# Seven block products for eight in w_out and w_down, and the norms behind them with half tiles between the transposes

## The reference

```python
merged = (jax.nn.sigmoid(ga) * jnp.einsum("bsc,cd->bsd", attn, w_attn_branch[l])
          + jax.nn.sigmoid(gc) * jnp.einsum("bsc,cd->bsd", conv, w_conv_branch[l]))
h = h + jnp.einsum("bsd,de->bse", merged, w_out[l])
hn = rms_norm(h, ffn_norm[l])
up = causal_depthwise_conv(jnp.einsum("bsd,df->bsf", hn, w_up[l]), ffn_conv_w[l])
gate, val = jnp.split(up, 2, axis=-1)
h = h + jnp.einsum("bsf,fd->bsd", jax.nn.silu(gate) * val, w_down[l])
return rms_norm(h, final_norm)
```

## Time and profile before

| what | value |
|---|---|
| runs | 1052.18, 1052.56, 1054.4 us, median 1052.56 |
| span of the profiled execution | 1050.5 us |
| time of the profiled execution around its span | not listed; the median of the runs is 2.06 us above the span |
| PE busy | 1038.4 us |
| DVE busy | 593.9 us |
| ACT busy | 445.9 us |
| POOL busy | 51.0 us |
| DMA traffic | 107.08 MB |

### The profile page before, as it was taken

One profiled execution on the slowest core, in us unless ns is written; L12 is line 12 of the kernel. 1 busy time (PEld: TensorE's weight loads), 2 busy tenths in 40 slices (PEclk: granted clock), 3 DMA queues, 4 the chain that ended last, 5 costly groups with the idle time before them and its releaser, 6 DMA issues.

```text
span 1050.5 us, 13952 instructions
## 1 busy us (share of the span) xinstructions
PE 1038.4 (99%) x5453; PEld 846.1 (81%) x5453; DVE 593.9 (57%) x1110; ACT 445.9 (42%) x855; POOL 51.0 (5%) x71
## 2 busy tenths in 40 slices
PE   9999999999999999999999999999999999999997
PEld 7877778888888888888888888899888677777785
DVE  6466665445356666533466563553456673567757
ACT  5355542233345434431234442453244454556640
POOL 0000000000001100000000000125200001000000
PEclk9999999999999999999999999999999999999999
DMA  7421133222341842333122323334211222511012
GB/s 277 160 65 57 61 101 100 95 89 98 123 140 41 275 152 87 98 125 110 61 101 85 100 97 110 131 122 135 91 61 61 61 81 71 211 41 41 21 61 80
DMA packets 29106, 107.08 MB, mean 102 GB/s; under 512 B 3227, under 2 KB 3371, under 8 KB 28401
## 3 DMA queue, kind: packets, MB, share of 16 engines
q1 hardware_dynamic: 24864, 86.13, 24.8%
q0 software_dynamic: 4032, 19.96, 5.3%
q10 hardware_dynamic: 144, 0.10, 0.0%
HBM read 101.44 MB, written 7.36 MB: 104 GB/s over the span
## 4 chain that ended last, share of the span: by engine, by line
PE 88%; DVE 5%; ACT 4%; issue 2%; DMA 2%; DVEq 0%; SPq 0%; ACTq 0%
PE ps L780 26%; PE ps L782 25%; PE ps L781 25%; PE ps L1054 2%; PE ps L1222 2%; PE ps L1205 1%; PE ps L1187 1%; DMA raw<-wp 1%; ACT whi L1285 1%; PE ps L1143 1%; PE ps L1106 1%; ACT SC L1336 1%; PE ps L1175 1%; DVE wlo L1633 0%; DVE SC L1739 0%
## 5 line engine op out<-in xcount | busy, mean ns | idle before, releaser
L780 PE MATMUL ps<-XH,whi 128*128 128x512 f32 (+1 forms) x864 | 336.7, 390 | 0.6 <-DVE XL L1646 0.2
L782 PE MATMUL ps<-XH,wlo 128*128 128x512 f32 (+1 forms) x864 | 326.9, 378 | 0.0
L781 PE MATMUL ps<-XL,whi 128*128 128x512 f32 (+1 forms) x864 | 326.5, 378 | 0.0
L1633 DVE TENSOR_TENSOR wlo<-raw,whi 128x1024 fp32r<-128x1024 f32 (+1 forms) x158 | 191.6, 1218 | 166.7 <-ACT whi L1285 166.1
L1285 ACT CAST whi<-raw 128x1024 fp32r<-128x1024 f32 (+1 forms) x158 | 161.2, 1027 | 95.9 <-PE ps L782 70.5
L780 PEld LDWEIGHTS ps<-XH,whi 128*128 128x128 f32 x864 | 162.6, 188 | 43.0 <-issue 12.4
L782 PEld LDWEIGHTS ps<-XH,wlo 128*128 128x128 f32 x864 | 162.6, 188 | 31.2
L781 PEld LDWEIGHTS ps<-XL,whi 128*128 128x128 f32 x864 | 162.8, 188 | 27.8 <-issue 0.5
L780 PE MATMUL ps<-whi,GH 128*128 128x512 f32 x176 | 68.8, 391 | 0.0
L782 PE MATMUL ps<-whi,GL 128*128 128x512 f32 x176 | 68.5, 389 | 0.0
L781 PE MATMUL ps<-wlo,GH 128*128 128x512 f32 x176 | 68.5, 389 | 0.0
(11 more groups left out here) (305 smaller groups left out, 1333.1 us busy)
## 6 DMA issues: line engine op xcount, KB each, us to landing
raw<-wp SPq DMA_DIRECT2D x150, 512.0 KB, 3.5
vec_dram<-row_dram POOLq DMA_DIRECT2D x1, 3072.0 KB, 13.7
H<-x POOLq DMA_DIRECT2D x1, 2048.0 KB, 8.1
x_dram<-H POOLq DMA_DIRECT2D x1, 2048.0 KB, 8.8
A<-w1c POOLq DMA_DIRECT2D x2, 1024.0 KB, 6.3
A<-x_dram POOLq DMA_DIRECT2D x1, 2048.0 KB, 12.8
y<-A SPq DMA_DIRECT2D x8, 256.0 KB, 2.0
raw<-wp SPq DMA_DIRECT2D x4, 402.0 KB, 3.9
```

What stands on the lines that cost most here:

```text
L780: self.e.matmul(o, ah, bh, start=start, stop=False)
L781: self.e.matmul(o, ah, bl, start=False, stop=False)
L782: return self.e.matmul(o, al, bh, start=False, stop=stop)
L1633: self.e.tensor_tensor(wlo[BUF[i]][:, 0:w], raw[i % NR][:, 0:w], whi[BUF[i]][:, 0:w].bitcast(F), ALU.subtract).then_inc(sems["lo"], 1)
```

## The change

The product of w_out (group 0) and that of w_down, now in three groups of 8, 8 and 6 feature tiles (groups 1, 2, 3), are each cut into 2 x 2 blocks: token halves, alternate feature tiles, column halves. By a scheme with seven block products in place of eight, the operands of some products are sums of blocks. DVE makes the sums of activations in halves of 256 tokens (`sums_of`), ACT and DVE split them into MW or GW, which hold seven operands. The sums of weight blocks come from accumulating DMAs that POOL issues into X and Y buffers (`wino_sums`); products 0, 3 and 4 take their blocks from SP's ring as before. The order of operand and target of each product is in `OPERAND`, `WBANKS`, `INTO`; products 2, 4 and 5 go on accumulating in the banks of 0, 1 and 2, and DVE adds or subtracts the bank to H behind each (behind product 5 to two parts of it).

In the groups with a norm (0 and 3), rows 0 and 1 are complete after product 4, the second column half of rows 2 and 3 after product 5, and the first after product 6. Their norms and transposes stand between the halves of products 5 and 6; behind product 6 the half tile of up slot 0, the transposes of row block 2, the half tile of slot 1, the transposes of row block 3 and the half tile of slot 2 alternate. whi and wlo have five buffers in turn here, and some more at the norms. In SBUF, Y0 (group 0) lies on the first half of XL.

The diff, cut to its core (memory layout, semaphore counts and the packing of weights on the host are left out):

```diff
+N_UNITS = 14
+SLOT_FFN = SLOT_WOUT + N_UNITS
+TILES_OF = [0, 8, 8, 6]
+PAIRS = [4, 4, 4, 3]
+FIRST_F = [0, 0, 8, 16]
+UNIT0 = [SLOT_WOUT] + [SLOT_FFN + 2 * (FIRST_F[G] + TILES_OF[G]) + N_UNITS * (G - 1) for G in (1, 2, 3)]
+LAST_G = 3
+SLOT_B2 = UNIT0[LAST_G] + N_UNITS
...
+OPERAND = [0, 4, 5, 1, 6, 3, 2]
+WBANKS = [(6, 7), (3, 0), (6, 7), (4, 5), (3, 0), (6, 7), (4, 5)]
+INTO = [(0, 0), (1, 1), (0, 1), (0, 0), (0, 1), (1, 1), (1, 0)]
+BEFORE = [(1, 3), (1, 5), (1, 4), (0, 0), (0, 2), (0, 1), (0, 5)]
...
+def added(G, p, r):
+
+    return 16 * G + (2 * p + r + 1 if p < 5 else 12 + 2 * r if p == 5 else 15 + r)
...
 def weave(main, *lanes):
@@ -226,19 +272,46 @@
     def slot(i):
         en.split_all(min(i + 3, N_SLOTS))
 
-    def rows_normed(m, rows):
-        for t in range(3):
-            rows(t)
-            if t == 2:
-                en.turn(m, 0)
-            en.norm_rest(m, t)
+    def product(G, p):
+        u = unit(G, p, 0)
+        en.split_all(u + 4)
+        en.wino(G, p, 0)
+        en.split_all(u + 5)
+        en.wino(G, p, 1)
+
+    def group(G):
+        product(G, 0)
+        product(G, 1)
+        en.wino_sums(G, 2)
+        product(G, 2)
+        en.wino_sums(G, 3)
+        product(G, 3)
+
+    def group_normed(G, m):
+        group(G)
+        product(G, 4)
+        u = unit(G, 6, 0)
+        en.split_all(u + 2)
+        en.eps_on(m, 0)
+        en.eps_on(m, 1)
+        en.wino(G, 5, 0)
+        en.norm_rest(m, 0)
+        en.wino(G, 5, 1)
+        en.norm_rest(m, 1)
+        en.eps_on(m, 2)
+        en.eps_on(m, 3)
+        en.split_all(u + 4)
+        en.wino(G, 6, 0)
+        en.turn(m, 0)
         en.turn(m, 1)
-        rows(3)
+        en.split_all(u + 5)
+        en.wino(G, 6, 1)
+        en.norm_rest(m, 2)
         en.norm_rest(m, 3)
-        en.turn(m, 2)
 
     def first_three(m, i, tile, tiles):
         en.part(i, 0, 0)
+        en.turn(m, 2)
         en.part(i, 1, 0)
         en.turn(m, 3)
         en.part(i, 2, 0)
@@ -306,50 +379,59 @@
     weave(conv(), (attention(), 0, 19 / 24))
     en.lower()
     for n in range(8):
+        if n == 5:
+            en.wino_sums(0, 0)
         for j in range(2):
             slot(SLOT_GATE + 3 * n + j)
             en.gate(n, j)
+            if j == 0 and n and n % 2 == 0:
+                for part in range(2):
+                    en.merge_sums(n // 2 - 1, part)
         slot(SLOT_GATE + 3 * n + 2)
         for j in range(2):
             en.branch(n, j)
+        if n == 7:
+            en.begin_norm(1)
+            en.wino_sums(0, 1)
         en.merge(n)
-
-    en.begin_norm(1)
-    for c in range(2):
-        for g in range(4 if c == 0 else 2):
-            slot(SLOT_WOUT + 4 * c + g)
-            if c == 1 and g == 1:
-                en.split_all(SLOT_FFN + 2)
-            for t in range(4):
-                en.wout(c, g, t)
-    en.split_all(SLOT_FFN + 3)
-    rows_normed(1, lambda t: en.wout(1, 3, t))
+    for part in range(2):
+        en.merge_sums(3, part)
+
+    group_normed(0, 1)
 
...
     en.ffn()
-    for half in range(2):
-        for j in range(11):
-            if half == 0 and j == 0:
-                first_three(1, SLOT_FFN, en.up, [(0, 0, 0, 2), (0, 0, 1, 2), (0, 1, 0, 2)])
+    for G in (1, 2, 3):
+        last = FIRST_F[G] + TILES_OF[G] - 1
+        for f in range(FIRST_F[G], last + 1):
+            if f == last - 2:
+                en.wino_sums(G, 0)
+                en.wino_sums(G, 1)
+            if f == 0:
+                first_three(1, SLOT_FFN, en.up, [(0, 0, 2), (0, 1, 2), (1, 0, 2)])
                 en.distances()
             else:
-                for g in range(1 if half == 0 and j == 1 else 0, 2):
-                    slot(SLOT_FFN + half * N_HALF + 2 * j + g)
-                    en.up(half, j, g, 0)
-                    en.up(half, j, g, 1)
-            en.glu(half, j)
-            if half == 0 and j == 10:
+                for g in range(1 if f == 1 else 0, 2):
+                    slot(up_slot(f, g))
+                    if f == last and g == 1:
+                        en.split_all(unit(G, 1, 1) + 1)
+                    en.up(f, g, 0)
+                    en.up(f, g, 1)
+                    if g == 0 and f % 2 == 0 and f > FIRST_F[G]:
+                        for part in range(2):
+                            en.glu_sums(f // 2 - 1, part)
+            if f == NF - 1:
+                en.begin_norm(2)
+            en.glu(f)
+            if f == 3:
                 en.biases()
-        if half == 1:
-            en.begin_norm(2)
-        for c in range(2):
-            for g in range(6 if half == 0 or c == 0 else 3):
-                i = SLOT_FFN + half * N_HALF + 22 + 6 * c + g
-                slot(i)
-                if half == 1 and c == 1:
-                    en.split_all(i + (4, 5, 7)[g])
-                for t in range(4):
-                    en.down(half, c, g, t)
-    rows_normed(2, lambda t: en.down(1, 1, 5, t))
+        for part in range(2):
+            en.glu_sums(last // 2, part)
+        if G < LAST_G:
+            group(G)
+            for p in range(4, 7):
+                product(G, p)
...
         KCH = sb("KCH", [P, 32], FR, pr)
@@ -733,6 +837,31 @@
         GAINS = [None, GR2, FN]
         NORMED = [None, XS2, H]
...
-            def wout(self, c, g, t):
-                if c:
-                    self.wait_ge("sq", sums_at(1, t, 0))
-                for gg in ((2, 3) if c == 1 and g == 3 else (g,)):
-                    self.rows(SLOT_WOUT + 4 * c + gg, t, MH, ML, 512, 2 * gg, range(2 * gg, 2 * gg + 2), 8,
-                              ("ml", lambda k: k + 1))
+            def wino(self, G, p, r):
+                t, n = WBANKS[p][r], OPERAND[p]
+                W = GW if G else MW
+                if p == 0:
+                    self.wait_ge("res", added(G - 1, 5, r))
+                    self.wait_ge("tt", 32)
+                    self.wait_ge("cp", 16)
+                elif p == 3:
+                    self.wait_ge("res", added(G - 1, 6, r))
+                elif p == 1:
+                    if G == 0:
+                        self.wait_ge("bm", 16)
+                        self.wait_ge("rsc", SCALED_GATE + 16)
+                    else:
+                        self.wait_ge("ub", 4 * (FIRST_F[G] + TILES_OF[G]))
+                        self.wait_ge("ve", 1)
+                    self.wait_ge("res", added(G - 1, 4, r))
+                else:
+                    self.wait_ge("res", added(G, {2: 0, 4: 1, 5: 2, 6: 3}[p], r))
+                at = 16 + 2 * FIRST_F[G] if G else 0
+                ts = slice(r * P, (r + 1) * P)
+                for s in range(2):
+                    i = unit(G, p, s)
+                    self.wait_ge("hi", i + 2)
+                    self.wait_ge("lo", i + 2)
+                    for m in range(2 * s, min(2 * s + 2, PAIRS[G])):
...
             def split(self, i):
-                self.wait_ge(f"w{i % NR}", 16 * (i // NR + 1))
+                self.wait_ge(*ready(i))
                 self.wait_ge("used", PREV[i] + 1)
-                if SLOT_FFN <= i < SLOT_FFN + 4:
-                    self.wait_ge("used", SLOT_WOUT)
-                    self.wait_ge("ml", 8)
+                if SLOT_WOUT <= i < SLOT_FFN:
+                    if PREV[i] < 0:
+                        self.wait_ge("used", SLOT_WOUT)
+                elif BUF[i] in (5, 9):
+                    self.wait_ge("used", unit(0 if i < SLOT_B2 else LAST_G, 3, 1) + 1)
                 elif BUF[i] == 6:
                     self.wait_ge("m", 32)
                 elif BUF[i] > 6:
                     self.wait_ge("n_tt", 72)
                     self.wait_ge("n_sc", 72)
                 w = WIDTH[i]
-                self.e.copy(whi[BUF[i]][:, 0:w], raw[i % NR][:, 0:w]).then_inc(sems["hi"], 1)
+                self.e.copy(whi[BUF[i]][:, 0:w], source(i)[:, 0:w]).then_inc(sems["hi"], 1)
                 self.splits = i + 1
 
             def split_all(self, n):
...
+            def wino(self, G, p, r):
+                if G in (0, LAST_G) and p in (3, 4, 5, 6):
+                    half, c = INTO[p]
+                    self.wait_ge("res", added(G, p, r))
+                    if G == 0:
+                        self.wait_ge("gl", 16)
+                    else:
+                        self.wait_ge("gl", 60)
+                    self.square(2 if G else 1, 2 * half + r, c, p in (4, 6), (UA if G else GA)[:, 0, 0, :])
 
...
             def eps_on(self, m, t):
@@ -1700,6 +1873,25 @@
                 a = st[:, at:at + 1]
                 self.wait_ge("sq", sums_at(m, t, 0))
                 self.e.tensor_scalar(a, a, 1.0 / D, 1e-5, ALU.mult, ALU.add).then_inc(sems["eps"], 1)
+
+            def wino(self, G, p, r):
+                half, c = INTO[p]
+                h = H[:, 2 * half + r, c * 512:c * 512 + 512]
+                if r:
+                    self.wait_ge("used", unit(G, p, 1) + 1)
+                else:
+                    self.wait_ge("tm", 3 + 7 * G + p + 1)
+                self.wait_ge("xn", 16)
```

(84 more changed lines are left out.)

407 lines of the change are left out of this document (244 added, 163 removed).

## The result

The changed kernel takes **1071.98 us** (median of 4 runs, 1069.42 to 1075.04) against 1053.24 us for the kernel before in the same session: the ratio is 1.0179, 95% interval 1.0158 to 1.0199. The forecast was 1057. The direction was right, the size was not: +18.7 us where +4.4 stood. The profiled execution took 1071.54 us, with a span of 1069.7.

The account below looks back on a forecast made before the run. PE's queue was taken to set the end. On the profiled span 1050.5 - 20.4 - 0.75 + 2 + 10.1 + 14.0 = 1055.5; the median, 2.06 above, was taken as 1057 us, range 1046 to 1068.

Parts of the forecast that it names:

- Removed matmuls, -20.4: Both changed products on PE: 630 matmuls for 720, 90 fewer at 0.2267 us each, -20.4 us.
- The norm chains, +10.1 and +14.0: Groups 0 and 3, product 3 to first half tiles: DVE and ACT make PE wait, +10.1 and +14.0 us.
- The loop: Groups 0 and 3, from product 3: addition, square, cast, subtraction take 3.55 us per half product, about 2.6 with 512-wide slots.
- For groups 1 to 3 they start tiles ahead and have over 30 us: nothing.: POOL's accumulating DMAs for weight-block sums in groups 1 to 3 start early enough to cost nothing.
- Y0, +2: Group 0, product 1: Y0's loads, sums and splits come 0.5 to 3 us late, taken as +2.
- Rival C: Accumulating DMAs take 10 us and over, delaying group 0's product 1 and product 5's split: 1065; chance 0.10.
- Rival D: PE's clock falls from 2.4 to 1.2 GHz after its waits, four slow half tiles, +11.6: 1069; chance 0.08.
- Rivals A and B: A: norm chains fit beside PE, 1033, chance 0.07. B: the chain binds only from product 5, 1048, chance 0.15.

Follow-up runs that it names:

- x_best: x_tail with DVE's and ACT's work around the norm put in the order in which PE asks for it: 1047.99 us, ratio 0.9943.
- x_fill: Changed kernel with spare PE matmuls before product 1 of group 0 and before the two turns of each norm: 1070.59 us, ratio 1.0157.
- x_hold: Changed kernel; POOL's last X sum waits for the ring's load for product 4's second slot, group 0's product 3 loads for Y0: 1057.83 us.
- x_y0: Changed kernel with product 1 of group 0 reading X0 in place of Y0, so its output differs: 1065.69 us, ratio 1.0112.
- x_plain: Changed kernel with POOL's accumulating DMAs made plain loads of the same blocks, so its output differs: 1058.18 us, ratio 1.0035.
- x_early: Changed kernel with the split of the slot two products on placed ahead of the squares in products 3 and 4, squares' scratch doubled: 1062.91 us.
- x_order: x_best with the two DMA holds of x_hold taken out: 1055.26 us (10 runs), ratio 1.0018.
- x_norm: Changed kernel with row blocks 0 and 1 normed ahead of product 5's additions, row 2 ahead of product 6's second: 1068.72 us, ratio 1.0153.
- x_tail: x_hold, x_early and x_norm combined, with XH and XL of rows 0 and 1 ahead of product 6's addition, one up-slot split moved: 1057.03 us.
- x_eh: Changed kernel with the edits of x_hold and x_early together: 1059.81 us, ratio 1.0057.
- x_pool: Changed kernel with only POOL's wait of x_hold, without SP's wait in group 0: 1062.79 us, ratio 1.0091.

## Why the prediction was wrong in size

- **Removed matmuls, -20.4.** Right: 90 fewer. With the order mended, in x_best, 2.9 us of group 0's 5.4 show: so much shorter than before is the stretch from w_out to the half tile.
- **The norm chains, +10.1 and +14.0.** Right in mechanism, and near in size. The loop is 3.55 and 2.59 us. The waits before turn 0 and turn 1 were to be about 2.35 and 3.0: they are 2.26 and 2.75 in group 0, 2.94 and 1.87 in group 3. The third, before the half tile, was to be about 3: only 0.53 us of it is idle, but PE spends 2.2 more in transposes and matmuls at half clock, which the forecast did not have. The sum comes out all the same, because DVE sets the half tile's start at either clock (x_fill). In x_hold, with the DMAs out of the way, the stretches come out at 51.2 and 364.2 us for 51.8 and 364.1. The step also said that order, not amount, was the cause: x_best, with the same instructions, shows it.
- **"For groups 1 to 3 they start tiles ahead and have over 30 us: nothing."** This is the step that failed. The sums do arrive in time; the question left out was what they do to the ring's loads beside them. Those land after 9.2 us instead of 3.5, ACT's cast for product 4's second slot waits 7.1 to 10 us in every group, and DVE and PE behind it. In groups 1 and 2 PE waits 2.6 us in all. In group 3 the first addition of product 3 comes 13.0 us after PE's wait for GW, in x_hold 9.2. In group 0 it comes 5.2 us after PE began the product, where the forecast had 2.95 and x_hold has 2.9.
- **Y0, +2.** The same cause, and a term too small: idle 4.04 and 0.19 us, and 6.3 by x_y0 with what follows. The range given there, 0.5 to 3, came from a sum at 3.5 to 7 us. The medians of all POOL's transfers, 6.3 and 7.1, would be near that, but the two sums that count landed after 8.0 and 9.2 us, and 6.2 where SP's loads were held back. The matmuls at half clock behind the wait, 1.6 us, were not in the term.
- **The whole miss** of 14.2 us in the span: 0.9 ahead of w_out, 5.0 up to the first half tile (Y0 and the late ring load), 6.3 up to the second (the ring's loads), and 2.0 behind it. x_hold, which only holds transfers back, ends 0.2 us above the forecast's span; x_plain, without the adding, 1.1 below it. No run ties the 0.9 and the 2.0 to the sums; 1.6 of the latter is the half clock of the last section.
- **Rival C** (sums at 10 us and over, 1065) named the right resource: Y0's sums came near its 10 us. What it left out is the path by which the rest was lost, delayed loads of the ring. **Rival D** happened: the clock falls to its half level after these waits, as the Trainium skill ("TensorE: Matmul & The Clock Gate", the part on the clock gate) lets one expect; this trace agrees, with 0.50 in 324 to 330 us. But D's price, 11.6 us, was added up as if PE set the end there. Behind a wait that another engine sets, slow matmuls use up time in which PE would wait: the 7.94 and 7.95 us under x_fill show it for both norms, and only the 1.6 us behind Y0 are left. **Rivals A and B** are excluded by the waits.
- The Trainium skill ("Collectives: The Full Stack", the section on the bandwidth ceiling) puts an adding transfer at half the rate. Measured from issue to landing at the same place and size: 7.1 against 5.2 us and 6.3 against 4.7, a factor of 1.35; the measurement decides. Neither figure says what the transfers do to the ring's loads beside them.

Open: why Y0 landed earlier in x_early, and why x_order's runs scatter by 7 us.

## What to carry to other kernels

When work moves into DMAs, ask not only whether its results come in time but whose loads run beside them: here two waits that hold transfers back gave 14 us, without an instruction less. When two engines feed a third, write each one's queue in the order in which the third asks; a square ahead of a cast turned 2.7 us of work into a loop of 3.55, and each re-ordering that only moved the knot (x_norm, x_tail) gave 1 to 3 us, hardly more than the scatter, while the one that undid it gave 10. Price a lower clock only where the engine that slows down sets the end.

## What the runs showed of the hardware that was not expected

An adding DMA of 512 KB on POOL's queue lands in 6.3 to 7.1 us, a plain one at the same place in 4.7 to 5.2, one on SP's queue in 3.5; and while POOL's are under way, SP's take 9.2 (median of three, 430 to 448 us).

The clock also fell once where PE had not waited: the changed kernel's timeline of PE, 53 us behind its last wait. Just before it stand 24 matmuls of only two columns each.

```profile
756.92 2.73 PE L1174 MATMUL ps<-H,A 128*128 128x2 f32 x24
...
760.42 0.63 PE L909 MATMUL ps<-whi,XH 128*128 128x512 f32 x1
760.84 0.63 PE L910 MATMUL ps<-wlo,XH 128*128 128x512 f32 x1
...
763.40 0.48 PE L910 MATMUL ps<-wlo,XH 128*128 128x512 f32 x1
```

Eight matmuls start 0.43 us apart, 1.6 us lost. Each of the kernels has these 24 matmuls, but the clock falls behind them in only seven of the fourteen profiled executions: the changed kernel, x_best (at 739.4), x_order, x_eh (748.2), x_early, x_pool and x_tail. In the kernel before, x_hold and the others it stays up. So these matmuls alone don't bring it on; what does stays open. It makes up most of the last stretch's 2.0 us over the forecast, and two profiled spans can differ by these 1.6 us alone.
